# Cached keys turned in 32x32 blocks on VectorE and moved by transfers inside the chip, with a new order in the expert stream and in the sample softmax

## The chip, the cores and the metric

The kernel runs on one core of one Trainium2 chip, as one launch. The metric is the device time in microseconds (us) of that core. Three runs of the kernel before gave 1206.78, 1207.28 and 1207.90 us; their median is 1207.28.

## The reference, cut to what matters

One decoder layer for 256 prompt tokens and 8 sample tokens (one per sequence), width 1024, all in float32. Per layer: sparse attention beside a pooling mixer, cross-attention into 256 memory tokens, and a top-4-of-32 mixture of experts, each added to the residual.

```
# sample group, per sequence: 2048 cached keys in 16 pages, one new key
ki_past = cache_idx_k[page_table].reshape(DB, past, IDX_DIM)
s       = einsum('bqhd,bsd->bqhs', qi, ki) * IDX_DIM ** -0.5
score   = einsum('bqh,bqhs->bqs', w, relu(s))        # indexer score of each key
_, sel  = top_k(score, 256)                          # keys that may be attended
p       = softmax(where(valid, q . k[sel] * HEAD_DIM ** -0.5, NEG))
attn    = p @ v[sel]

# experts, for all 264 tokens
h    = tok @ w_up[e] + b_up[e]                       # 1024 x 2048 per expert
gate = minimum(h[:, :D], 7);  up = clip(h[:, D:], -7, 7)
out  = (gate * sigmoid(1.702 * gate) * (up + 1)) @ w_down[e] + b_down[e]
acc += combine[e][:, None] * out                     # combine is 0 where e is not in the top 4
```

The weights of an expert are 8 MiB (up) and 4 MiB (down); all 32 experts are computed.

## The kernel before, in words

Each engine has a program of its own, in an order written out by hand, and waits for the others on semaphores. Results of TensorE go to eight PSUM banks that are handed out in turn by the list `psum_jobs`: a job takes its bank (`take`) when the job eight places ahead of it has been copied out (`drained`), and announces its own end (`filled`). The order of that list is the order of TensorE's program.

**The front (0 to 280 us).** `w_in` is loaded in eight pieces, the seven projection tiles of `Z_FIRST` are computed, then the others (`z_tile`), each rotated by VectorE with the help of a swapped copy (`swap_halves` on TensorE, `rotate` on VectorE). Beside it the cached keys are made ready. A gather on GpSimd's queue (L623) brings a quarter `q` of the cached keys and indexer keys (two of 1 MiB) into `raw`; GpSimd copies the two side by side into `both` (L644, L646); TensorE turns `both` with 32 transposes of 128x128 per quarter (`turn_keys`, L782); ScalarE copies eight PSUM banks per quarter into `KT` (`keep_keys`). `sample_logits(c)` (L793) multiplies a quarter of the keys with the query heads, ScalarE takes the rectified values (`RL`) and the logits (`LG`), `sample_score(c)` (L801) sums the heads into scores, which ScalarE copies into `XS`. VectorE meanwhile finds the top 64 keys of each prompt token (accumulation at L1876 and L1878, then rounds of L1890 and L1892, first for token tile t = 0, then for t = 1, up to L1895), takes the prompt logits (L1919, L1928), and when all of `XS` is there, starts at L1964 a search for the 256th score in eight rounds (L1978), each with a small count on TensorE (L814). From its result `drop` a mask is spread over the heads by TensorE (`mb`, L966), added to the logits (L2010); one reduction over 2049 keys gives the maximum (L2019), one ScalarE instruction the exponentials with their sum (L1595), VectorE multiplies with the reciprocal (L2021, L2022), TensorE turns the probabilities (`spT`, L997) and multiplies them with the values (`spv`), and the output product `wo` (L1033), the memory attention and the router follow.

**The expert stream (from 280 us).** The weights of an expert come in six parts of 2 MiB (parts 0 to 3 up, 4 and 5 down). A ring of ten buffers (`RING`) holds them; the first ten parts are loaded during the front, wherever a buffer comes free. SyncE loads part `use + 10` when TensorE has read part `use` (`part_read`, `up_full`, `down_full`; L557 and L561 are the issues). TensorE's `expert` runs the up product (`up_rows`, L1258), gathers the next tokens (`gather_prompts`, L1201), turns the activations (L1236), adds the biases and sample tokens (L1209, L1215), runs the down product (`down_rows`, L1295) with the turned next tokens (L1223) inside it. Once per pair of experts, `spread_rows(0)` and `spread_rows(1)` (L1245) bring the finished rows of the pair before back to their tokens; they stand behind parts 0 and 1 of the even expert's up product, and VectorE adds them in `add_rows` (L2226), ahead of `activate`. `last_expert` turns the residual between its parts and spreads the rows of the expert before the last (`spread_before_last`, L1344), for tile r = 2 (8 rows) just ahead of the last down product. VectorE and ScalarE then norm and write the three tiles.

Of the kernel before, what the change touches and what calls it, by code (L numbers as in the profile page):

```python
# [25 lines left out]
P = 128  # L26
# [6 lines left out]
HD = 64  # L33
# [124 lines left out]
def psum_jobs():  # L158
    js = [("xT", k) for k in range(KD)]
    js += [("z", m) for m in Z_FIRST] + [("rs",)]  # L160
    js += [("z", 1), ("sw", 13), ("sw", 9), ("kin",), ("wr",)] + [("kt", i) for i in range(4)]
    js += [("z", 2), ("sw", 10), ("sw", 11)] + [("kt", i) for i in range(4, 8)]
    js += [("z", 3), ("sw", 12), ("sw", 4), ("sw", 0), ("kvn",), ("z", 5), ("sw", 1), ("sw", 2), ("sw", 3)]
    js += [("kt", i) for i in range(8, 12)] + [("is", 0, g, o) for g in range(2) for o in range(2)]
    js += [("z", 6)] + [("kt", i) for i in range(12, 16)] + [("is", 1, g, o) for g in range(2) for o in range(2)]
    js += [("z", 7), ("z", 8)]
    js += [("sl", 0)] + [("kt", i) for i in range(16, 24)]
    js += [("sl", 1), ("sc", 0)] + [("kt", i) for i in range(24, 32)]
    js += [("sl", 2)] + [("lg", 0, g, o) for g in range(2) for o in range(2)]
# [28 lines left out]
def build(nc, ins, outs, consts, ybuf):  # L198
# [6 lines left out]
    with ExitStack() as ctx:  # L205
# [119 lines left out]
        both = unit(14, 32, 2 * HD)  # L325
        KT = [unit(8, P, 32), unit(10, P, 32)]
# [174 lines left out]
        def _(sp):  # L501
# [26 lines left out]
            w_mk_rows = w_mk[0].rearrange("(k p) h e -> p k (h e)", p=P)  # L528
            wait_filled(sp, "sl", 3)
# [20 lines left out]
            load(vm, cache_mem_v[0].rearrange("b (t p) h e -> p b t (h e)", p=P), "vm_in")  # L550
            def load_part(use, e):
# [49 lines left out]
            for use in range(2):  # L601
                part_read(loops * BODY, use)
                load_part(use + RING, e)
# [12 lines left out]
        def _(pool):  # L616
# [12 lines left out]
            for q in range(4):  # L629
                gather(raw[:, 0].rearrange("p t d -> p (t d)"), cache_k, q, "raw_k")  # L630
                gather(raw[:, 1].rearrange("p t d -> p (t d)"), cache_idx_k, q, "raw_i")
                if q == 3:
                    wait_filled(pool, "z", 8)
                    for part in range(4):
                        gather(v_raw[:, 32 * part:32 * part + 32, :].rearrange("p t d -> p (t d)"), cache_v, part,
                               "raw_v")
                if q == 0:
                    for k in range(KD):
                        wait_filled(pool, "xT", k)
                else:  # L640
                    wait_filled(pool, "kt", 8 * q - 1)
# [5 lines left out]
                pool.wait_ge(S("side_by_side"), 2 * q + 2)  # L647
# [47 lines left out]
        def _(pe):  # L695
# [79 lines left out]
            def turn_keys(i):  # L775

                q = i // 8
                if i % 8 == 0:
                    pe.wait_ge(S("side_by_side"), 2 * q + 2)
                b = take(pe, "kt", i)  # L780
                for j in range(4):
                    ins = pe.transpose(b[:, j * P:(j + 1) * P], both[:, (4 * i + j) % 32, :], ident)  # L782
                done(ins, "kt", i)

            def sample_logits(c):
                for i in range(8 * c, 8 * c + 8):
                    wait_drained(pe, "kt", i)
                b = take(pe, "sl", c)
                for s in range(2):
                    for b4 in range(4):  # L790
                        n = 4 * s + b4
                        keys = KT[c % 2][:, n * NPG:(n + 1) * NPG, :].rearrange("p g t -> p (g t)")
# [25 lines left out]
            swap_halves(9)  # L818
            b = take(pe, "kin")
# [8 lines left out]
            for i in range(4):  # L828
                turn_keys(i)
            z_tile(2)  # L830
            swap_halves(10)
            swap_halves(11)
            for i in range(4, 8):
                turn_keys(i)
# [3 lines left out]
            swap_halves(0)  # L838
            b = take(pe, "kvn")
# [5 lines left out]
            z_tile(5)  # L845
            for m in (1, 2, 3):
                swap_halves(m)
            for i in range(8, 12):
                turn_keys(i)
# [5 lines left out]
            for i in range(12, 16):  # L855
                turn_keys(i)
            head_products("is", qiT, kiT, ki2, 1)
            z_tile(7)
            z_tile(8)
            pe.wait_ge(S("qb_ready"), 6)  # L860
            sample_logits(0)
            for i in range(16, 24):
                turn_keys(i)
            sample_logits(1)
            sample_score(0)
            for i in range(24, 32):
                turn_keys(i)
# [561 lines left out]
        def _(act):  # L1429
# [74 lines left out]
            for m in Z_FIRST + [1]:  # L1504
                keep_z(m)
# [818 lines left out]
```

## Time and profile before

| | us |
|---|---|
| median of three runs | 1207.28 |
| the profiled execution | 1206.73 |
| its span, first to last instruction | 1204.9 |
| PE busy | 1144.1 (95%) |
| DVE busy | 374.9 (31%) |
| ACT busy | 223.7 (19%) |
| POOL busy | 57.3 (5%) |
| mean granted TensorE clock | 0.995 |

PE is TensorE, PEld its weight loads, DVE VectorE, ACT ScalarE, POOL GpSimd, SP SyncE (SPq its DMA queue). A float32 matmul and a weight load count as two instructions each, a transpose as one. The device moved 451.92 MB, 374 GB/s over the span; in the slices from about 300 us to the end the page shows 426 to 430 GB/s, in those before 106 to 412 GB/s.

### The profile page before, as it was taken

How to read it: one execution, taken by the hardware profiler on the slowest of the kernel's cores; microseconds unless marked ns; L12 is line 12 of the kernel's file. 1: busy time of each engine (PE TensorE's matmuls, PEld its weight loads, DVE VectorE, ACT ScalarE, POOL GpSimd, SP SyncE). 2: the span in 40 equal slices, each digit the busy share in tenths (PEclk: the TensorE clock that was granted, in tenths of full speed). 3: DMA queues.
4: the chain of work that ended last, by engine and by line, in shares of the span. 5: the costliest groups of instructions: out<-in, count | busy, mean ns of one | idle time of the engine just before them, and what ended most of it. 6: DMA issues, size and time to landing. Idle time of an engine off the chain costs nothing.

```text
span 1204.9 us, 15008 instructions
## 1 busy us (share of the span) xinstructions
PE 1144.1 (95%) x5865; PEld 508.8 (42%) x5865; DVE 374.9 (31%) x888; ACT 223.7 (19%) x449; POOL 57.3 (5%) x71
## 2 busy tenths in 40 slices
PE   7998999999999999999999999999989898999997
PEld 6776568773333333333333333333323333333332
DVE  2279942534231322222222223122212222222222
ACT  2236641442111111111111111111111111111102
POOL 2138100000000000000000000000000000000000
PEclk9999999999999999999999999999999999999999
DMA  9345447797999999999999999999999999999994
GB/s 371 106 146 211 168 145 290 297 412 280 404 429 428 426 427 429 426 427 427 428 428 427 427 428 429 426 426 428 428 426 430 427 426 428 427 427 428 429 426 205
DMA packets 44245, 451.92 MB, mean 375 GB/s; under 512 B 5516, under 2 KB 6440, under 8 KB 18055
## 3 DMA queue, kind: packets, MB, share of 16 engines
q1 hardware_dynamic: 41695, 436.94, 86.7%
q0 software_dynamic: 2480, 14.02, 3.1%
q8 instruction: 47, 0.77, 0.3%
q14 instruction: 23, 0.19, 0.0%
HBM read 448.56 MB, written 2.61 MB: 374 GB/s over the span
## 4 chain that ended last, share of the span: by engine, by line
PE 59%; DMA 25%; DVE 12%; ACT 3%; issue 1%; SPq 0%; DVEq 0%; ACTq 0%
DMA mem<-in_w_up_dram 25%; PE psum L1258 20%; PE psum L1295 15%; PE psum L724 4%; PE psum L1245 3%; PE psum L1033 2%; DVE mem L2239 2%; PE psum L1209 2%; PE psum L931 1%; DVE mem L2231 1%; DVE mem L2234 1%; PE psum L1236 1%; ACT mem L1706 1%; DVE mem L2236 1%; PE psum L1223 1%
## 5 line engine op out<-in xcount | busy, mean ns | idle before, releaser
L1258 PE MATMUL psum<-mem 128*64 128x512 f32 x2048 | 457.4, 596 | 13.7 <-DMA mem<-in_w_up_dram 13.2
L1258 PEld LDWEIGHTS psum<-mem 128*64 128x64 f32 x2048 | 142.6, 137 | 303.8 <-issue 274.7
L1295 PE MATMUL psum<-mem 128*64 128x512 f32 x1024 | 236.9, 600 | 0.0
L1295 PEld LDWEIGHTS psum<-mem 128*64 128x64 f32 x1024 | 66.5, 136 | 133.2 <-issue 112.6
L2231 DVE TENSOR_SCALAR mem<-psum 128x512 f32<-128x512 f32 x32 | 22.2, 693 | 275.1 <-PE psum L1258 275.1
L1706 ACT ACTIVATE mem<-mem 128x512 f32<-128x512 f32 x32 | 20.2, 631 | 467.2 <-DVE mem L2231 467.2
L2226 DVE TENSOR_TENSOR mem<-mem,psum 128x528 f32<-128x528 f32 x64 | 45.2, 706 | 130.1 <-PE psum L1245 130.1
L1432 ACT ACTIVATE mem<-psum 128x512 f32<-128x512 f32 (+6 forms) x125 | 61.0, 550 | 97.6 <-PE psum L724 40.9
L1245 PE MATMUL psum<-mem 128*128 128x264 f32 x256 | 65.5, 398 | 0.0
L2216 DVE TENSOR_SCALAR mem<-mem 128x64 f32<-128x64 f32 x99 | 25.0, 312 | 126.9 <-PE psum L1230 99.4
L1201 PE MATMUL psum<-mem 128*64 128x512 f32 x256 | 60.4, 592 | 1.0 <-DVE mem L2147 1.0
L1245 PEld LDWEIGHTS psum<-mem 128*128 128x128 f32 x256 | 45.8, 188 | 32.5 <-issue 26.0
L724 PE MATMUL psum<-mem 128*128 128x264 f32 (+1 forms) x224 | 54.2, 403 | 0.7 <-DVE mem L1805 0.7
L2257 DVE COPY mem<-psum 64x512 f32<-64x512 f32 x30 | 20.5, 684 | 102.1 <-PE psum L1295 102.1
L724 PEld LDWEIGHTS psum<-mem 128*128 128x128 f32 (+1 forms) x224 | 43.2, 196 | 9.7 <-issue 1.1
L1716 ACT ACTIVATE mem<-psum 64x512 f32<-64x512 f32 x30 | 17.8, 595 | 118.7 <-PE psum L1295 118.7
L1708 ACT ACTIVATE mem<-psum 128x512 f32<-128x512 f32 x32 | 19.2, 599 | 104.3 <-PE psum L1236 104.3
L1236 PE MATMUL psum<-mem 128*128 128x128 f32 x128 | 21.0, 287 | 17.1 <-DVE mem L2239 17.1
L2239 DVE SCALAR_TENSOR_TENSOR mem<-mem 128x512 f32<-128x512 f32 x32 | 34.5, 1078 | 1.1
L1209 PE MATMUL psum<-mem 32*64 32x512 f32 x256 | 34.8, 613 | 0.0
L1215 PE MATMUL psum<-mem 8*64 8x512 f32 x128 | 34.4, 613 | 0.0
L1201 PEld LDWEIGHTS psum<-mem 128*64 128x64 f32 x256 | 18.3, 136 | 37.0 <-issue 37.0
(355 smaller groups left out, 859.8 us busy)
## 6 DMA issues: line engine op xcount, KB each, us to landing
mem<-in_w_up_dram SPq DMA_DIRECT2D x128, 2048.0 KB, 32.5
mem<-in_w_down_dram SPq DMA_DIRECT2D x64, 2048.0 KB, 33.8
mem<-in_w_in_dram SPq DMA_DIRECT2D x8, 868.0 KB, 15.5
mem<-in_cache_mem_k_dram SPq DMA_DIRECT2D x1, 4096.0 KB, 19.9
mem<-in_cache_mem_v_dram SPq DMA_DIRECT2D x1, 4096.0 KB, 15.0
mem<-in_w_o_dram SPq DMA_DIRECT2D x1, 3072.0 KB, 10.9
mem<-in_w_mk_dram SPq DMA_DIRECT2D x2, 1024.0 KB, 6.8
mem<-in_w_mv_dram SPq DMA_DIRECT2D x1, 2048.0 KB, 10.5
```

Source lines behind the costliest of these rows:

```text
L724: return pe.matmul(b[0:w, 0:NT], w_in_sb[k][:, m * P:m * P + w], xnT[:, k, :], start=(k == 0), stop=(k == KD - 1))
L1201: pe.matmul(psx[64 * o:64 * o + 64, :], slot_of[:, r, :], xn01[:, r, o * 512:(o + 1) * 512], start=(r == 0), stop=False, skip_group_check= ...
L1209: pe.matmul(ps[64 * o:64 * o + 64, :], esel[rows, :], ybias[rows, o * 512:(o + 1) * 512], start=True, stop=False, skip_group_check=True)
L1215: ins = pe.matmul(psx[64 * o:64 * o + 64, :], slot_of[0:TS, 2, :], etab[0:TS, o * 512:(o + 1) * 512], start=False, stop=True, skip_group_c ...
L1236: ins = pe.transpose(psa_t[:, c * P:(c + 1) * P], sig_b[:, c * P:(c + 1) * P], ident)
L1245: ins = pe.matmul(ps[:, 0:NT], outb[:, c * P:(c + 1) * P], ST[:, :], start=True, stop=True)
L1258: ins = pe.matmul(ps[64 * o:64 * o + 64, :], lhs, w[:, k % 2, g * 1024 + o * 512:g * 1024 + (o + 1) * 512], start=False, stop=(k == 7), sk ...
L1295: ins = pe.matmul(pso[64 * o:64 * o + 64, :], lhs, w[:, k % 4, o * 512:(o + 1) * 512], start=(k == 0), stop=(k == 7), skip_group_check=True)
L1432: ins = act.activation(out, in_, ACT.Copy)
L2226: dve.tensor_tensor(v, v, ps, ALU.add).then_inc(S("y_added"), 1)
L2231: dve.tensor_scalar(gate_b, banks[3], 7.0, None, ALU.min).then_inc(S("gate_ready"), 1)
L2239: dve.scalar_tensor_tensor(out=sig_b.rearrange("p (c q) -> p c q", c=4), in0=act_b.rearrange(turned, c=4), scalar=1.0, in1=gate_b.rearrang ...
```

## The change

1. **Keys.** `both`, GpSimd's eight copies, TensorE's 128 transposes and ScalarE's 32 copies go. `turn_blocks(q)` on VectorE turns each quarter of `raw` in 32x32 blocks into `blocks` (two instructions of 128x2048), and SyncE's queue moves it into `KT` with sixteen transfers per quarter, each of 32 partitions x 4 KiB, from partitions 32g to partitions 32b. `turn_blocks(0)` stands ahead of `rotate(13)`, (1) behind `rotate(9)`, (2) behind the copies into `QB`, (3) between the two prompt tiles of the top-64 search. The gather of quarter q waits for the blocks of q-1, the blocks of q wait for the transfers of q-1. TensorE's list is put in another order, with `sample_logits(0)` and `(1)` ahead of `z_tile(7)`.
2. **Sample softmax.** The maximum is taken in the four mask additions, the exponentials come in four pieces, TensorE turns each piece without waiting for the reciprocal, and ScalarE applies the reciprocal when it copies out the product with the values.
3. **Expert stream.** The spreads of finished rows go from parts 0 and 1 of the even expert's up product to behind the first and the second half of its down product (in the body; the last even expert keeps them: `early=True`). Biases and sample tokens are placed ahead of the turned activations, the turned next tokens ahead of the down product. The very first load of each pass of the body waits for half a part only (`row_read`) and comes in two halves; the last part comes in two halves with a semaphore of its own for the second. `spread_before_last(2)` goes behind the last down product.

```diff
+            for q in range(4):                                   # SyncE
+                sp.wait_ge(S("keys_turned"), 2 * q + 2)
+                if q >= 2:
+                    wait_filled(sp, "sl", q - 2)
+                for b4 in range(4):
+                    for g in range(4):
+                        sp.dma_start(KT[q % 2][32 * b4:32 * b4 + 32, g], blocks[32 * g:32 * g + 32, b4]
+                                     ).then_inc(S("keys_moved"), 16)
             wait_filled(sp, "sl", 3)
...
             for q in range(4):                                   # GpSimd
+                if q:
+                    pool.wait_ge(S("keys_turned"), 2 * q)
                 gather(raw[:, 0].rearrange("p t d -> p (t d)"), cache_k, q, "raw_k")
                 gather(raw[:, 1].rearrange("p t d -> p (t d)"), cache_idx_k, q, "raw_i")
-                pool.wait_ge(S("raw_k"), 16 * q + 16)
-                pool.tensor_copy(both[:, :, 0:HD], raw[:, 0]).then_inc(S("side_by_side"), 1)
-                pool.wait_ge(S("raw_i"), 16 * q + 16)
-                pool.tensor_copy(both[:, :, HD:2 * HD], raw[:, 1]).then_inc(S("side_by_side"), 1)
...
             def sample_logits(c):                                # TensorE
-                for i in range(8 * c, 8 * c + 8):
-                    wait_drained(pe, "kt", i)
+                pe.wait_ge(S("keys_moved"), 256 * (c + 1))
...
+            def turn_blocks(q):                                  # VectorE
+                for kind, name in enumerate(("raw_k", "raw_i")):
+                    dve.wait_ge(S(name), 16 * q + 16)
+                    if q:
+                        dve.wait_ge(S("keys_moved"), 256 * q)
+                    dve.transpose(blocks[:, 2 * kind:2 * kind + 2],
+                                  raw[:, kind].rearrange("p t (b d) -> p b t d", b=2)).then_inc(S("keys_turned"), 1)
...
-                dve.scalar_tensor_tensor(out=v, in0=v, scalar=HD ** -0.5, in1=b[:, :], op0=ALU.mult, op1=ALU.add
+                dve.tensor_tensor_reduce(v, v, b[:, :], HD ** -0.5, -FMAX, ALU.add, ALU.max, stat[:, 36 + c:37 + c]
...
-            act.activation(LG, LG, ACT.Exp, bias=stat[:, 0:1], accum_out=stat[:, 2:3]).then_inc(S("exp_s"), 1)
+            for c in range(4):
+                v = LG[:, c * 512:(c + 1) * 512 if c < 3 else NKEY]
+                act.activation(v, v, ACT.Exp, bias=stat[:, 0:1], accum_out=stat[:, 41 + c:42 + c]).then_inc(S("exp_s"), 1)
...
-            dve.tensor_scalar(LG, LG, stat[:, 2:3], None, ALU.mult).then_inc(S("prob_s_ready"), 1)
...
+                    if use == 0:                                 # SyncE, in the loop over the experts
+                        sp.wait_ge(S("row_read"), j + 1)
+                        load_half(later, e, 0, "slot0_in")
+                        part_read(j * BODY, 0)
+                        load_half(later, e, 1, "slot0_in")
+                        continue
...
             def expert(j, i, n, pair, early=False):              # TensorE
                 up_product(j, i, n, pair, early)
+                if i % 2 == 1 or early:
                     pe.wait_ge(S("y_added"), pair * 4 + 4)
                 gather_prompts(n + 2)
+                pe.wait_ge(S("gate_ready"), n + 1)
+                pe.wait_ge(S("up_clipped"), n + 1)
+                bias_rows()
+                gather_samples()
                 pe.wait_ge(S("act_ready"), n + 1)
                 turn_activations()
-                bias_rows()
-                gather_samples()
+                turn_tokens(n + 2)
                 pe.wait_ge(S("actt_copied"), n + 1)
-                down_part(j, i, 0, (0, 1))
-                turn_tokens(n + 2)
-                down_part(j, i, 0, (2, 3))
+                down_part(j, i, 0, (0, 1, 2, 3))
                 if i % 2 == 1:
                     turn_slots(gated)
+                elif not early:
+                    pe.wait_ge(S("xet_copied"), n + 2)
+                    finished_rows(n, pair, 0)
                 down_part(j, i, 1, (4, 5, 6, 7))
+                if i % 2 == 0 and not early:
+                    finished_rows(n, pair, 1)
...
-                down_part(j, 1, 1, (4, 5, 6, 7))                 # last expert
+                down_part(j, 1, 1, (4, 5))
+                pe.wait_ge(S("last_half_in"), 16)
+                down_part(j, 1, 1, (6, 7))
```

## Rows read from the trace of the kernel before

**Rows 1.** page part 4: shares of the span by line
```profile
DMA mem<-in_w_up_dram 25%; PE psum L1258 20%; PE psum L1295 15%; PE psum L724 4%; PE psum L1245 3%; PE psum L1033 2%; DVE mem L2239 2%; PE psum L1209 2%; PE psum L931 1%; DVE mem L2231 1%; DVE mem L2234 1%; PE psum L1236 1%; ACT mem L1706 1%; DVE mem L2236 1%; PE psum L1223 1%
```

**Rows 2.** chain of waits in order: start us, length us, what
```profile
338.45 3.43 PE psum L1258 x16
...
394.24 3.43 PE psum L1258 x16
...
1077.51 42.49 DMA mem<-in_w_up_dram
...
1136.25 43.09 DMA mem<-in_w_up_dram
```

**Rows 3.** DMA view: totals of 280:320, then of 320:360 us
```profile
DMA packets 851, 12.50 MB, mean 313 GB/s; under 512 B 87, under 2 KB 87, under 8 KB 87
...
DMA packets 1185, 17.11 MB, mean 428 GB/s; under 512 B 141, under 2 KB 141, under 8 KB 141
```

**Rows 4.** timeline of PE, first expert: start us, us, what, xcount
```profile
280.76 5.33 PE L1258 MATMUL psum<-mem 128*64 128x512 f32 x16
...
286.02 2.05 PE L1245 MATMUL psum<-mem 128*128 128x264 f32 x8
...
300.48 1.89 PE L1201 MATMUL psum<-mem 128*64 128x512 f32 x8
...
304.52 1.94 PE L1295 MATMUL psum<-mem 128*64 128x512 f32 x8
```

**Rows 5.** timeline of SP's DMA queue, 0 to 345 us
```profile
36.46 0.82 SPq L503 DMA_DIRECT2D out_dram<-in_state_pool_dram  x1
...
286.28 5.89 SPq L561 DMA_DIRECT2D mem<-in_w_down_dram  x2
```

**Rows 6.** timeline of PE, the last expert
```profile
1186.82 1.03 PE L1344 MATMUL psum<-mem 64*8 64x512 f32 x4
...
1187.77 7.09 PE L1295 MATMUL psum<-mem 128*64 128x512 f32 x32
```

**Rows 7.** DMA view, 1184:1194 us, GB/s in slices of 0.25 us
```profile
GB/s 377 213 131 459 131 328 197 328 279 98 410 229 279 279 66 197 246 246 213 279 49 49 66 16 33 16 33 0 0 0 0 0 0 0 0 0 0 0 0 0
```

**Rows 8.** timelines of PE and DVE in the sample softmax
```profile
162.83 5.42 PE L931 MATMUL psum<-mem 128*128 128x512 f32 x12
...
166.77 1.29 DVE L2022 TENSOR_SCALAR mem<-mem 128x2049 f32<-128x2049 f32 x1
```

**Rows 9.** timeline of DVE in the front
```profile
45.20 0.43 DVE L1823 TENSOR_TENSOR mem<-mem 8x264 f32<-8x264 f32 x1 [21.84 <-PE psum L741]
...
92.67 2.01 DVE L1895 SCALAR_TENSOR_TENSOR mem<-mem 128x128 f32<-128x128 f32 x1
...
110.00 2.34 DVE L1964 TENSOR_SCALAR_CACHE_REDUCE mem<-mem 128x2049 f32<-128x2049 f32 x1
```

**Rows 10.** waits of DVE, 45.2 to 110 us: us in total, times, longest
```profile
DVE mem L1825 <- PE psum L741: 10.9, 3, 4.3
...
DVE mem L1876 <- ACT mem L1501: 4.0, 1, 4.0
```

**Rows 11.** timeline of PE in the front
```profile
104.13 1.92 PE L793 MATMUL psum<-mem 128*32 128x512 f32 x16
```

**Rows 12.** page group of DVE over 2049 keys
```profile
L1978 DVE TENSOR_SCALAR_CACHE_REDUCE mem<-mem 128x2049 f32<-128x2049 f32 x7 | 16.4, 2349 | 0.3
```

**Rows 13.** b_up loads: GB/s in 65 ns slices from 148.4; landing
```profile
GB/s 441 441 315 315 504 378 189 0 0 0 252 63 189 504 315 63 315 441 126 252 189 252 63 315 189 189 189 252 0 0 0 0 0 0 0 0 0 0 0 0
...
DMA to landing us min/median/max: 2.4/2.4/2.5
```

**Rows 14.** PE by form, 14:16 and 30:38; clock ahead of DMA share, 282
```profile
L724 PE MATMUL psum<-mem 128*128 128x264 f32 x6 | 2.8, 647 | 0.0
...
L724 PE MATMUL psum<-mem 128*128 128x264 f32 x32 | 7.6, 386 | 0.0
...
282.00:283.00 1.00, 1.00 (x4) 0.24 (x2) 0.86 (x6) 0.93 (x1) 0.00 (x0) 0.50 0.09 25
```

More of the change, by code:

```diff
@@ L324, in build @@
         raw = unit(16, 2, 32, HD)
-        both = unit(14, 32, 2 * HD)
-        KT = [unit(8, P, 32), unit(10, P, 32)]
+        blocks = unit(14, 4, 32, 32)
+        KT = [unit(8, 4, 32, 32), unit(10, 4, 32, 32)]
         prob = [at(home(8), NH, P), at(home(8) + 1024, NH, TP)]
@@ L854, in _ @@
             z_tile(6)
-            for i in range(12, 16):
-                turn_keys(i)
             head_products("is", qiT, kiT, ki2, 1)
+            pe.wait_ge(S("qb_ready"), 6)
+            sample_logits(0)
+            sample_logits(1)
             z_tile(7)
             z_tile(8)
[L860 to L867, printed above, removed]
             sample_logits(2)
@@ L1261, in up_rows, with finished_rows, up_product @@
                 return ins
-            def up_product(j, i, n, pair):
+            def finished_rows(n, pair, half):
+                if half == 0:
+                    pe.wait_ge(S("rows_out"), n + 1)
+                    pe.wait_ge(S("rows_out2"), n + 1)
+                else:
+                    pe.wait_ge(S("y_added"), pair * 4 + 2)
+                spread_rows(half)
+            def up_product(j, i, n, pair, spreads):
                 pe.wait_ge(S("xet_copied"), n + 1)
@@ L1415, in _ @@
                     expert(j, i, j * BODY + i, j * (BODY // 2) + i // 2)
-            expert(loops, 0, loops * BODY, loops * (BODY // 2))
+            expert(loops, 0, loops * BODY, loops * (BODY // 2), early=True)
             last_expert(loops, loops * BODY + 1, loops * (BODY // 2))
@@ L1508, in _ @@
             copy(kin[0:TS, 2, :], b[0:TS, 144:216], "kin")
-            for i in range(4):
-                keep_keys(i)
-            keep_z(2)
-            for i in range(4, 8):
-                keep_keys(i)
             keep_z(3)
+            keep_z(5)
             b = result(act, "kvn")
@@ L1528, in _ @@
             keep_logits(0)
-            for i in range(16, 24):
-                keep_keys(i)
             keep_logits(1)
             keep_scores(0)
-            for i in range(24, 32):
-                keep_keys(i)
             keep_logits(2)
@@ L1706, in expert @@
                 act.activation(sig_b, gate_b, ACT.Sigmoid, scale=1.702).then_inc(S("sig_ready"), 1)
+                if not last:
+                    copy_tokens(n + 2)
                 act.wait_ge(S("actt_full"), n + 1)
@@ L1898, in _ @@
                     link(ins)
+                    turn_blocks(3)
                 else:
@@ L2245, in expert @@
                 e = dve.value_load(item_e[0:1, bass.ds(n + 2, 1)], min_val=0, max_val=NE - 1)
-                if b == 0:
-                    for m in range(4):
-                        add_rows(pair, m)
                 activate(n)
@@ L2255, in expert @@
                 assign_slots(n + 3, e)
+                if b == 0:
+                    add_rows(pair, 0)
+                    add_rows(pair, 1)
+                    dve.wait_ge(S("y_full"), pair * 4 + 4)
                 dve.wait_ge(S("down_full"), n + 1)
                 dve.tensor_copy(outb[64 * b:64 * b + 64, 0:512], banks[5][0:64, :]).then_inc(S("rows_out"), 1)
+                if b == 0:
+                    add_rows(pair, 2)
+                    add_rows(pair, 3)
             dve.wait_ge(S("list_ready"), 3)
```

136 lines of the change are left out of this document (59 added, 77 removed).

## The prediction

> **What bounds the kernel now.** I read the shares by line first: the largest step of the chain is the load of the up weights, and the products L1258 and L1295 come next, so the expert stream is the place [rows 1]. In the chain in order of time the reader is to see two regimes [rows 2]. From 338.45 to 394.24 us a pair of experts takes 55.8 us and every step is TensorE's. Late in the stream nearly a whole pair is one DMA step, and a pair takes 58.7 us (1077.51 to 1136.25): 12 parts of 2 MiB in 58.7 us are 428 GB/s. The DMA view shows that this rate is already there at 320 to 360 us [rows 3]. So the queue is full all the time; TensorE only lives on the ten parts loaded ahead until they are used up. What sets the end is (a) when the stream starts, (b) how long its queue runs empty in the first experts, (c) what follows the last up part, which lands at 1136.25 + 43.09 = 1179.3. A faster TensorE between 320 and 1130 us is worth nothing. From 280 to 320 us 12.50 MB moved, 29.2 us at 428 GB/s; so the queue ran as if it had started at 290.8 and never paused. Ahead of 280 us everything hangs on one serial chain; a shift s of it shifts all that comes later by s.
>
> **Expert stream.** The first part is read for 5.33 us and the first load goes out at 286.28 [rows 4, 5]. Now half a part is enough. These 16 instructions ran partly at the low clock (below), so I put their middle at 284.3, not at 283.4; the stream starts 1.9 us earlier. Then each spread of 2.0 us leaves parts 0 and 1, two in all [rows 4], so the parts 1, 2, 3 come free 2.0, 4.0, 4.0 us earlier, and the fourth the same. With 4.9 us of transfer per part (2.10 MB at 428) I ran through it: starts at 285.1, 290.6, 295.5, 300.4, 305.3, then 310.7 for the part that comes free at the end of the first down half (L1295 starts at 304.52 now, at 300.8 then) and the next; pauses 0.6 + 0.5 + 0.5 = 1.6 us. The stream is then as good as started at 285.1 + 1.6 = 286.7 instead of 290.8: **-4.1 us**. Bounds: 0 (the freed time is not used) and -5. The order inside `expert` (biases early, turned tokens ahead of the down product) is worth some 0.3 us of TensorE per expert, hidden behind the DMA queue: 0. The spreads in the down product and the later `add_rows` cost the same 4 us per pair as before; they sit behind `down_full` of the half that was read, so the queue is full when they come: 0. Only a pair of over 58.7 us would bring them into the sum, 3 us more than now.
>
> **Tail.** The last down product starts at 1187.77, behind a spread of 8 rows of 1.03 us [rows 6] that goes behind it: -0.95. It comes back in part, since tile 2 is then ready about when ScalarE wants it: +0.1. The last part lands before 1190.7, where the GB/s row falls to zero [rows 7]. Its first half would be wanted at 1190.4 and its second at 1192.1; with the two halves this fits. **-0.85**, bounds -1.0 and +0.5 (waits for the half).
>
> **Sample softmax.** Removed from VectorE: one pass for the maximum and one of 1.29 us for the scale. But behind the mask TensorE runs without a pause to 168.25 us on the memory values, then turns memory keys, and only then the probabilities, which were ready at 168.06 already [rows 8]. So the saving is off the path. VectorE now copies three of the four turned banks, ScalarE one: **-0.2**, bounds -0.6 and +0.5.
>
> **Keys.** This decides s. Before, VectorE reaches the search at 110.00 [rows 9], just when ScalarE copies the last score; both paths end together. Now they part.
>
> VectorE's path. From 45.20 to 110.00 it waited 14.9 us for TensorE's swapped tiles and for ScalarE [rows 10]; these go, as TensorE has 128 transposes less in that stretch, but 1.5 us of new waits for products I leave in. GpSimd's copies held VectorE three times: L1895 over 128 columns took 2.01 us instead of 0.35 [rows 9]; I count three such stalls (80.0, 92.7, 94.7), 4.9 us, gone. Added: three times two instructions over 2048 elements (the first quarter's two fit in the idle 21.84 us ahead of 45.20). No row shows a transpose; the nearest are 1.29 us (a multiply) and 2.35 us (a compare with a sum) per 2049 elements [rows 8, 12]. I take 2.2: 13.2 us; at 1.29 it would be 7.7. The Trainium skill says (Vector Engine (DVE) Microarchitecture Reference, on the reshape front end) that the 32x32 transpose sustains one element per cycle per lane; no run here shows it yet. The second quarter's blocks also wait for the first quarter's transfers: these go out at 37.3, when SP's queue is through [rows 5], and land at 49.4 (11.1 us as worked out below, and 1 us for the gather still under way) against 48.6, where `rotate(9)` ends: +0.8. Sum: 110.0 - 14.9 - 4.9 + 13.2 + 1.5 + 0.8 = 105.7. So VectorE alone would be 4.3 us earlier.
>
> The keys' path. Behind the fourth quarter's blocks VectorE has what it had from 94.7 to 110.0, less a stall: 13.8 us. So these blocks are done at 91.9. Then sixteen transfers of 128 KiB. No row has a transfer inside the chip of that size. The nearest are the two of `b_up`, also 32 partitions x 4 KiB: issued at 0.4 us each, 0.26 MB in 1.17 us (slices 11 to 28), so 224 GB/s, half the stream's 428; the first byte 1 us behind the issue, the landing 0.7 us behind the last [rows 13]. A quarter of 2.10 MB takes 9.4 + 1.7 = 11.1 us. At 428 GB/s it would be bound by the issues: 15 x 0.4 + 2.4 = 8.4 us. At half of `b_up`'s rate, if reading and writing the same SBUF count twice: 20.4 us. I take 11.1, and 1.5 us for the 4 MiB of values gathered at that time. A rule speaks against the change here: the Trainium skill (SBUF — State Buffer, Door 1: The DMA port swizzle) says that a run of 32 partitions reaches only half of the DMA ports, about 218 GB/s, and that transfers to the two halves in flight together hardly gain. The trace's 224 agrees; by the rule the quarter takes 11.3 us, by the full rate 8.4.
>
> So the keys are there at 91.9 + 11.1 + 1.5 = 104.5, hardly later than L793 starts now, 104.13 [rows 11], and from there 5.9 us to the search. But TensorE has been idle for over 10 us by then, and it wakes slowly: in 14 to 16 us, after the idle start, L724 took 647 ns, later 386; and at 282 us the granted clock was 0.50, that is 1.2 GHz, after the short waits for VectorE behind the router [rows 14]. The path holds 4.3 us of TensorE work, so between 0 and +4.3; I take +2.8, and 0.5 more for the values turned behind it. Search at 104.5 + 5.9 + 3.3 = 113.7: **s = +3.7**. From there on the chain is what it was. What goes on TensorE, ScalarE and GpSimd is not on this path.
>
> **Sum.** 3.7 - 4.1 - 0.85 - 0.2 = -1.45 us on the profiled execution of 1206.73: 1205.3. The median is 0.55 above that execution: **1205.8**.
>
> **Rivals.** Each is worked from the same sum.
> - Full rate: the transfers run at 8.4 us. Then no wait at 48.6 either, keys at 91.1 + 8.4 + 1.0 = 100.5, search at 109.7, s = -0.3: 1201.8. For it: sixteen transfers go to different partitions. Against: `b_up`. The same size of gain comes if the transpose costs 1.29 (s lower by 5.5: 1200.3); against it, that only plain one-input passes run that fast.
> - Slower than before: the transfers take more than 12.55 us per quarter, since s = T - 7.4 and 5.15 are to be paid back; more than 15 us is slower by over 2.4. Above 15 us VectorE itself starts to wait for the quarter before, three times over. At 20.4 us the four quarters run one behind the other: blocks 1 at 58.7, 2 at 83.5, 3 at 108.3, keys at 134.6, search at 143.8, s = +33.8: 1235.9. For it: source and target are the same memory, and gathers of 2 and 4 MiB share the queues. Against: nothing in the rows is under 200 GB/s at that shape.
> - The stream keeps its late start (the queue's pauses have another cause, or the half load saves nothing): -1.45 + 4.1: 1209.9. Against: the issue at 286.28 follows the end of part 0.
>
> **How the numbers follow.** My forecast has 0.50, with 1202.5 to 1209.5 as its own range (clock and shared queues, 3.5 us each way). Full rate or quick transpose 0.26, slow transfers 0.14, late stream 0.10. A measurement tells 0.2%, 2.4 us, from no change. Forecast: 0.13 faster, 0.30 same, 0.07 slower; full rate: 0.25 faster, 0.01 same; slow transfers: 0.14 slower; late stream: 0.02 faster, 0.04 same, 0.04 slower. Together 0.40, 0.35, 0.25. The range leaves out the slow end beyond 15 us and the best of the quick cases: 1199.5 to 1213.
>
> **What would show it.** In the trace after: the transpose's mean (2.2 us); the transfers' time from issue to landing and the GB/s of their stretch (some 220); the last `turn_blocks` ending near 92; L793's fourth run starting near 104.5 and taking more than 1.92 us at a low clock; the search starting near 113.7; the first load 2 us earlier behind the first product; 428 GB/s from then on; pairs of 58.7 us at the end; the last down product right behind the turned activations. I am wrong if the search starts ahead of 110, if the load stream is not at 428 GB/s, or if a pair takes over 59 us.

## The result and the profile after

Four runs of the changed kernel gave 1217.54, 1220.24, 1220.63 and 1220.68 us, median 1220.43, beside 1207.35 of the kernel before: a ratio of 1.0101, 95% interval 1.0086 to 1.0116. The change makes the kernel 12.2 us slower by this ratio (10.4 to 14.0), 13.1 by the medians. I had forecast 1205.8.

The profiled execution is the one of 1217.54 us, with a span of 1215.7 us, 10.8 more than before. Shares of the span by line; they answer to [rows 1] and look almost alike, which shows only that the stream still ends the kernel:

```profile
DMA mem<-in_w_up_dram 28%; PE psum L1249 21%; PE psum L1291 14%; PE psum L1233 4%; PE psum L1189 3%; SPq L532 3%; SPq L500 3%; PE psum L1021 2%; DMA mem<-mem 2%; PE psum L1197 2%; PE psum L919 1%; PE psum L1211 1%; PE psum L1135 1%; PE psum L1040 1%; ACT mem L1667 1%
```

New in it is SyncE's queue with L532, the sixteen transfers per quarter. VectorE's timeline in the front, kernel after (start us, length us, what, and in brackets the idle time before it with what ended it); it answers to [rows 9]:

```profile
51.34 4.50 DVE L1837 STREAM_TRANSPOSE mem<-mem 128x2048 f32<-128x2048 f32 x2 [4.64 <-DMA mem<-mem]
...
74.57 4.50 DVE L1837 STREAM_TRANSPOSE mem<-mem 128x2048 f32<-128x2048 f32 x2 [5.71 <-DMA mem<-mem]
...
100.58 4.50 DVE L1837 STREAM_TRANSPOSE mem<-mem 128x2048 f32<-128x2048 f32 x2 [6.56 <-DMA mem<-mem]
...
127.08 2.35 DVE L1971 TENSOR_SCALAR_CACHE_REDUCE mem<-mem 128x2049 f32<-128x2049 f32 x1 [8.33 <-ACT mem L1438]
```

Three times VectorE stands still, 16.9 us in all, until the transfers of the quarter before have landed. The fourth blocks are done at 105.1, and the search begins at 127.08: s = +17.1, where I had +3.7. TensorE's four runs of L793 and SyncE's queue in the same stretch; they answer to [rows 11] and [rows 5]:

```profile
72.49 1.93 PE L793 MATMUL psum<-mem 128*32 128x512 f32 x16
...
80.46 3.64 PE L793 MATMUL psum<-mem 128*32 128x512 f32 x16 [6.05 <-ACT mem L1502]
...
100.50 3.37 PE L793 MATMUL psum<-mem 128*32 128x512 f32 x16 [7.92 <-DMA mem<-mem]
...
120.05 3.64 PE L793 MATMUL psum<-mem 128*32 128x512 f32 x16 [13.17 <-DMA mem<-mem]
```

```profile
37.15 78.88 SPq L532 DMA_DIRECT2D mem<-mem  x64
...
299.77 1.89 SPq L560 DMA_DIRECT2D mem<-in_w_down_dram  x2
```

A quarter's transfers, from the turned blocks (for the first, from SyncE's first issue at 37.15) to their use, take 14.2, 18.8, 21.5 and 15.0 us. I had 11.1, and 12.6 for the fourth. The windows of 2 us in the first quarter (last three columns: granted clock, DMA share, GB/s) show the DMA engines full at half of the stream's rate:

```profile
40.00:42.00 2.00, 2.00 (x10) 1.71 (x10) 0.00 (x0) 0.00 (x0) 0.00 (x0) 1.00 0.92 210
42.00:44.00 2.00, 2.00 (x9) 1.13 (x9) 0.62 (x2) 0.39 (x1) 0.00 (x0) 1.00 1.02 213
44.00:46.00 2.00, 2.00 (x11) 1.71 (x10) 1.90 (x7) 0.00 (x0) 0.00 (x0) 1.00 0.99 213
```

The rest went as forecast or better. TensorE at the start of the stream and at its end, answering to [rows 4] and [rows 6]:

```profile
297.50 13.95 PE L1249 MATMUL psum<-mem 128*64 128x512 f32 x64
...
1197.62 1.04 PE L1338 MATMUL psum<-mem 128*8 128x128 f32 x8
1198.59 7.09 PE L1291 MATMUL psum<-mem 128*64 128x512 f32 x32
1206.47 1.99 PE L1429 MATMUL psum<-mem 64*128 64x512 f32 x8 [0.79 <-DVE mem L2295]
1208.39 1.03 PE L1346 MATMUL psum<-mem 64*8 64x512 f32 x4
```

The first product starts 16.7 us later than before and runs through without the spread that stood in it. The first load goes out 2.3 us behind its start, not 5.5. The last down product stands right behind the turned activations.

### The profile page after: what moved, and what is told of

The parts are those of the page before. It is cut to its first block, busy times and chain, and to the rows that moved or that the text cites. A ratio compares the mean times of both kernels' runs of the same rounds, so it can differ in the third digit from the quotient of the medians.

```text
span 1215.7 us, 14858 instructions
## 1 busy us (share of the span) xinstructions
PE 1133.2 (93%) x5736; PEld 499.1 (41%) x5737; DVE 381.9 (31%) x902; ACT 205.6 (17%) x422; POOL 40.7 (3%) x63
## 4 chain that ended last, share of the span: by engine, by line
PE 56%; DMA 30%; SPq 6%; DVE 4%; ACT 2%; issue 2%; DVEq 0%; ACTq 0%
DMA mem<-in_w_up_dram 28%; PE psum L1249 21%; PE psum L1291 14%; PE psum L1233 4%; PE psum L1189 3%; SPq L532 3%; SPq L500 3%; PE psum L1021 2%; DMA mem<-mem 2%; PE psum L1197 2%; PE psum L919 1%; PE psum L1211 1%; PE psum L1135 1%; PE psum L1040 1%; ACT mem L1667 1%
## 5 line engine op out<-in xcount | busy, mean ns | idle before, releaser
L1249 PEld LDWEIGHTS psum<-mem 128*64 128x64 f32 x2048 | 143.8, 137 | 318.8 <-issue 271.3
L1291 PEld LDWEIGHTS psum<-mem 128*64 128x64 f32 x1024 | 68.3, 137 | 121.6 <-issue 117.1
L1438 ACT ACTIVATE mem<-psum 128x512 f32<-128x512 f32 (+7 forms) x91 | 43.8, 529 | 103.2 <-PE psum L735 47.4
L1710 ACT ACTIVATE mem<-psum 64x512 f32<-64x512 f32 x30 | 17.8, 593 | 206.0 <-PE psum L1233 158.0
L735 PEld LDWEIGHTS psum<-mem 128*128 128x128 f32 (+1 forms) x224 | 43.4, 196 | 11.1 <-issue 2.4
L793 PE MATMUL psum<-mem 128*32 128x512 f32 x64 | 12.6, 929 | 27.1 <-DMA mem<-mem 21.1
L1189 PEld LDWEIGHTS psum<-mem 128*64 128x64 f32 x256 | 18.4, 137 | 37.0 <-issue 37.0
## 6 DMA issues: line engine op xcount, KB each, us to landing
mem<-in_w_o_dram SPq DMA_DIRECT2D x1, 3072.0 KB, 11.6
```

The costliest lines, as they stand in the source:

```text
L735: return pe.matmul(b[0:w, 0:NT], w_in_sb[k][:, m * P:m * P + w], xnT[:, k, :], start=(k == 0), stop=(k == KD - 1))
L1189: pe.matmul(psx[64 * o:64 * o + 64, :], slot_of[:, r, :], xn01[:, r, o * 512:(o + 1) * 512], start=(r == 0), stop=False, skip_group_check= ...
L1249: ins = pe.matmul(ps[64 * o:64 * o + 64, :], lhs, w[:, k % 2, g * 1024 + o * 512:g * 1024 + (o + 1) * 512], start=False, stop=(k == 7), sk ...
L1291: ins = pe.matmul(pso[64 * o:64 * o + 64, :], lhs, w[:, k % 4, o * 512:(o + 1) * 512], start=(k == 0), stop=(k == 7), skip_group_check=True)
L1438: ins = act.activation(out, in_, ACT.Copy)
```

## The experiments

Two theories on the transfers. **Path:** 32 partitions at either end can take or give only about half of the full rate, so the DMA engines are full at 205 to 220 GB/s. **Issue:** SyncE needs 0.635 us for each of the 64 issues, and 131 KB in 0.635 us are 206 GB/s. In the change the two numbers are the same, so its trace can't tell them apart. Each experiment is the changed kernel with the edit shown, unless it says otherwise. In the table, the first quarter's transfers run from the first issue to their use; where VectorE no longer waits for them, to their landing (e7) or to where the DMA share falls to zero (e10). The search started at 110.00 before. In e4, e7, e8, e9 and e10 the keys are not the reference's (parts are left out, or the blocks don't get to their places), so they are measurements of time and no kernels to use.

| run | median us | ratio to before, 95% interval | first quarter's transfers us | search start |
|---|---|---|---|---|
| the change | 1220.43 | 1.0101 (1.0086 to 1.0116) | 14.2 | 127.1 |
| e1_old_keys | 1205.73 | 0.9984 (0.9973 to 0.9995) | none | 112.5 |
| e2_keys_only | 1224.03 | 1.0134 (1.0116 to 1.0153) | as the change | 127.8 |
| e3_mixed_order | 1212.02 | 1.0042 (1.0031 to 1.0054) | 12.0 | 121.1 |
| e4_half_bytes | 1203.40 | 0.9963 (0.9951 to 0.9976) | 11.6 | 111.1 |
| e5_two_queues_mixed | 1217.35 | 1.0084 (1.0055 to 1.0113) | 12.3 | 125.2 |
| e6_two_queues_same_order | 1222.55 | 1.0124 (1.0106 to 1.0143) | 12.5 | 131.6 |
| e7_whole_transfer | 1199.90 | 0.9940 (0.9921 to 0.9958) | 8.8 | 109.2 |
| e8_one_gather | 1204.62 | one run | not read | 114.3 |
| e9_four_narrow | 1218.11 | one run | 13.5 | 127.3 |
| e10_four_wide | 1202.54 | one run | 8.1 | 108.6 |
| e11_act_copies_share | 1204.58 | 0.9977 (0.9967 to 0.9986) | off the path | 112.7 |
| e12_act_copies_half | 1201.18 | 0.9956 (0.9943 to 0.9970) | off the path | 108.3 |

**The parts alone.** e1 is the kernel before with the stream's, the tail's and the softmax's edits; e2 is the kernel before with the keys' edits.

> The kernel before with the stream's, the tail's and the sample softmax's edits, the keys turned on TensorE as before. The trace of the change has the stream 4.9 us shorter, the tail 1.0 us, the softmax 0.35 us, against 17.1 us that the search begins later. If these are separate terms: 1207.3 - 6.2 = 1201.1 us (1200 to 1202.5), search start 110.0. Rival: the stream is shorter only because it begins late (less beside it, a full ring): then 1205 to 1207.

> The kernel before with the new way of the keys alone; stream, tail and softmax as before. Separate terms: 1207.3 + 17.1 = 1224.4 us (1222 to 1227), search start 127.1. If the transfers cost less than that by themselves and the rest of the change is what is slow: under 1217.

e2 came as expected: +16.2 us (14.0 to 18.5) where the shift of the search is 17.8. So the loss is the keys' alone. e1 gained 1.9 us (0.6 to 3.3), where I had 6.2: a miss, and its time lies in the range of the rival that I wrote beside it, that the stream is shorter only because it begins late. e2's trace refutes that rival: its first product starts at 298.71, 18.0 us later than before, and from there to the end it takes 924.3 us with the old stream, 924.1 before. More on e1 is below. The two add up to +14.3, the change measured +12.2; the intervals meet.

**Order and bytes.**

```diff
-                for b4 in range(4):
-                    for g in range(4):
+                for i in range(4):                               # e3_mixed_order
+                    for b4, g in ((0, i), (2, (i + 2) % 4), (1, (i + 1) % 4), (3, (i + 3) % 4)):
...
-    sp.dma_start(KT[q % 2][32 * b4:32 * b4 + 32, g], blocks[32 * g:32 * g + 32, b4])
+    sp.dma_start(KT[q % 2][32 * b4:32 * b4 + 32, g, 0:16], blocks[32 * g:32 * g + 32, b4, 0:16])   # e4_half_bytes
```

> The changed kernel with the 16 transfers of a quarter in another order: four that follow each other read four different groups of 32 partitions and write four different ones (before: four in a row write the same 32 partitions). Theory path (the 32 partitions at either end can only take or give about half of the full rate, so 131 KB last 0.62 us and the queue backs up): an issue falls from 0.635 us to the 0.4 us of a load of the same kind, a quarter's transfers from 14.2 to about 10.5 us, search start 127 -> 113 to 118, time 1206 to 1212 us. Theory issue (SyncE needs 0.635 us for each, whatever it moves): nothing changes, 1217 to 1221 us.

> The changed kernel, each of the 64 transfers with half its bytes (65 KB in 32 rows of 2 KB); the other half of the keys is zeros written once at the start by GpSimd, so the keys are not the reference's. Theory path: an issue follows the bytes, 0.3 to 0.4 us, a quarter 14.2 -> 8.5 to 10 us, search start 107 to 115, time 1201 to 1209 us. Theory issue: 0.635 us each still, first quarter 13 to 14.2 us, the later ones a little shorter (less beside the gathers), 1214 to 1220 us.

The lines of the transfers in the first quarter (duration of the issue in ns, least, median and most; then first and last start) of the change, e3 and e4, with the time from issue to landing where the view gives it:

```profile
L532 SPq DMA_DIRECT2D mem<-mem x16: 584/592/885, 37.1 to 47.0; - x16
```

```profile
L532 SPq DMA_DIRECT2D mem<-mem x16: 590/595/622, 37.2 to 46.8; - x16
...
DMA to landing us min/median/max: 2.3/2.4/3.5
```

```profile
L533 SPq DMA_DIRECT2D mem<-mem x16: 585/591/622, 37.0 to 46.5; - x16
...
DMA to landing us min/median/max: 2.0/2.0/3.2
```

Neither theory passes whole. e4 came in at the time of the path theory (1203.4 us), but its first quarter took 11.6 us for 8.5 to 10; e3 came in at the edge of that theory's time (1212.0) with 12.0 us for 10.5. The issue takes 0.59 us with half the bytes and in any order, so 15 x 0.635 + 2 = 11.5 us is a floor for sixteen issues from one queue. But with half the bytes the engines are only half busy:

```profile
42.00:44.00 2.00, 2.00 (x9) 1.16 (x8) 0.27 (x1) 0.39 (x1) 0.00 (x0) 1.00 0.45 106
44.00:46.00 2.00, 2.00 (x11) 1.71 (x10) 1.87 (x7) 0.00 (x0) 0.00 (x0) 1.00 0.45 108
```

So 106 GB/s cost 0.45 of the engines here, and the full bytes all of them. Where the gathers run beside the transfers, that is what counts: the second and third quarter fell from 18.8 and 21.5 us to 14.1 and 15.6, and the time by 17 us, while the first quarter fell by only 2.6. The order is worth 2.2 us in the first quarter, 7 to 8 us of time in all.

**Two queues.** In e5 and e6 ScalarE issues every second transfer, in the mixed order and in the change's.

```diff
+        def move_keys(eng, q, moves):              # SyncE: MOVES[0::2], ScalarE: MOVES[1::2]
+            eng.wait_ge(S("keys_turned"), 2 * q + 2)
...
             for m in Z_FIRST:
                 keep_z(m)
+            move_keys(act, 0, MOVES[1::2])
```

> The changed kernel with the mixed order of e3_mixed_order and every second transfer issued by ScalarE. So far: an issue holds SyncE 0.635 us whatever it moves and in whatever order (0.59 with half the bytes too), and the last of 16 lands 4.6 us after its issue in the change's order, 2.4 in the mixed one. If both are terms: first quarter 12.0 -> 8 x 0.635 + 2.4 = 7.5 us (7 to 9), later quarters 18.3, 19.1, 12.9 -> 12 to 14, 13 to 15, 8.5, search start 121.1 -> 112 or less, time 1212.0 -> 1202 to 1205 us. If two queues share what one has (the DMA engines take 32-row transfers at this rate, whoever issues): first quarter 11 to 12, 1211 to 1213 us.

> As e5_two_queues_mixed, but in the change's order (four in a row write the same 32 partitions). Theory path and issue together: the issue is over after 5 us, but 2.1 MB go to 32 partitions at a time at 205 to 220 GB/s, so the first quarter is 9.5 to 10.5 us + 2 = 11 to 12.5 us (was 14.2), time 1210 to 1215 us. Theory issue alone: as the mixed order, 7.5 us and 1202 to 1205 us.

e5 refutes the first of its two forecasts (7.5 us): two queues share the full DMA engines. With the issues shared, the transfers still go at 217 to 250 GB/s, and the first quarter takes 12.3 us, about as the second forecast had it. Windows of e5, then of e6:

```profile
40.00:42.00 2.00, 2.00 (x11) 1.71 (x10) 0.00 (x0) 0.21 (x1) 0.00 (x0) 1.00 0.97 240
42.00:44.00 2.00, 2.00 (x10) 1.13 (x9) 0.00 (x0) 0.00 (x0) 0.00 (x0) 1.00 0.99 217
44.00:46.00 2.00, 2.00 (x10) 1.71 (x11) 1.87 (x6) 0.00 (x0) 0.00 (x0) 1.00 0.96 250
```

```profile
42.00:44.00 2.00, 2.00 (x10) 1.34 (x9) 0.00 (x0) 0.00 (x0) 0.00 (x0) 1.00 1.00 260
44.00:46.00 2.00, 2.00 (x10) 1.50 (x9) 1.48 (x4) 0.00 (x0) 0.00 (x0) 1.00 1.00 266
```

e6's first quarter took 12.5 us, at the end of its range of 11 to 12.5, but its time is 1222.6 us, over the forecast 1210 to 1215: its later quarters are again slower than e5's, the second 20.3 us for 17.4.

e5's time also lies over its forecast of 1211 to 1213. It costs 5.3 us against e3, since ScalarE now stands in its issues while others wait for its copies. Its timeline in e5 shows eight issues in 6.2 us ahead of the rectified products that VectorE works on:

```profile
76.02 6.17 ACTq L504 DMA_DIRECT2D mem<-mem  x8
82.58 0.66 ACT L1508 ACTIVATE mem<-psum 128x256 f32<-128x256 f32 x2 [18.84 <-issue]
```

The values' gather went out at 94.9, not at 89.2 as in e3, and met the fourth quarter's transfers, which took 17.3 us, not 12.9.

**Width.** The same bytes in one transfer (e7), in four of 32 rows x 16 KB (e9), in four of 128 rows x 4 KB (e10).

```diff
-                for b4 in range(4):
-                    for g in range(4):
-                        sp.dma_start(KT[q % 2][32 * b4:32 * b4 + 32, g], blocks[32 * g:32 * g + 32, b4])
+                sp.dma_start(KT[q % 2], blocks)                                                  # e7_whole_transfer
...
+                for g in range(4):                                                               # e9_four_narrow
+                    sp.dma_start(KT[q % 2][32 * (3 - g):32 * (3 - g) + 32], blocks[32 * g:32 * g + 32])
...
+                for g in range(4):                                                               # e10_four_wide
+                    sp.dma_start(KT[q % 2][:, g], blocks[:, g])
```

> The changed kernel with one transfer of 128 rows x 16 KB for each quarter in place of 16 of 32 rows; the blocks stay in their groups of partitions, so the keys are not the reference's. 2.1 MB at 420 GB/s are 5.0 us, + 2.4 of landing: first quarter 7.4 us (14.2), search start 111 to 114, time 1202 to 1206 us. If a transfer inside the chip goes at half the rate of a load however wide it is: 10 + 2.4 = 12.4 us, 1210 to 1214 us.

> The changed kernel with four transfers for each quarter, each of 32 rows x 16 KB from one group of 32 partitions to another (the blocks land in another place than they belong, so the keys are not the reference's). Against 16 of 32 x 4 KB it has a quarter of the issues and rows four times as long, and is as narrow. Seen so far: 32 rows x 4 KB go at 205 to 250 GB/s with the DMA engines busy, from one queue or two; 128 rows x 16 KB at 377 GB/s. Theory path (32 partitions at either end are too narrow): 205 to 250 GB/s, the first quarter's transfers 10 to 12 us. Theory row (a row of 4 KB costs an engine too much beside its bytes): over 350 GB/s, 8 to 9 us as in e7_whole_transfer.

> As e9_four_narrow, but each of the four transfers takes 4 KB of all 128 partitions (128 rows x 4 KB). Theory path: wide, so over 350 GB/s, the first quarter's 8 to 9 us, time 1200 to 1203 us. Theory row: the rows are as short as the change's, so 205 to 250 GB/s, 10 to 12 us.

Windows of the first quarter, first e9, then e10:

```profile
42.00:44.00 2.00, 2.00 (x9) 1.15 (x8) 0.25 (x1) 0.39 (x1) 0.00 (x0) 1.00 1.07 229
44.00:46.00 2.00, 2.00 (x11) 1.71 (x10) 1.87 (x7) 0.00 (x0) 0.00 (x0) 1.00 1.07 229
```

```profile
40.00:42.00 2.00, 2.00 (x11) 1.71 (x10) 0.00 (x0) 0.12 (x1) 0.00 (x0) 1.00 1.02 414
42.00:44.00 2.00, 2.00 (x9) 1.16 (x8) 0.05 (x1) 0.39 (x1) 0.00 (x0) 1.00 0.94 377
```

Four issues of 32 rows run at 229 GB/s and give 1218.1 us, about as slow as the change, without its issues; four issues of 128 rows run at 377 to 414 GB/s, with the same 4 KB rows as the change, and give 1202.5. The path is what counts, its width in partitions, and neither the row's length nor that source and target are the same memory. (e9's first quarter took 13.5 us, over the 10 to 12 that I had for it; its rate was in the range.)

One rival is left by the edits: e7 and e10 keep every row on its own partition, e9 does not. No run moves 128 rows between groups of partitions. Two rows speak against it: `b_up` comes from memory and goes to 32 partitions at 224 GB/s [rows 13], and in the change 4 of the 16 transfers of a quarter stay in their own group, while no slice of 0.18 us between 42 and 49 us is over 281 GB/s. Which of the two ends is the narrow one, source or target, these runs don't separate; `b_up` shows that a narrow target alone is enough.

The Trainium skill says (SBUF — State Buffer, Door 1: The DMA port swizzle) that a run of 32 partitions reaches half of the ports; 229 against 377 to 414 GB/s agree. It also says (same page, "Can I just issue two DMAs to hit both halves?") that two transfers to both halves in flight together hardly gain; e5, where SyncE's transfers go to the lower half of the partitions and ScalarE's to the upper, moves 233 GB/s from 40 to 48 us, and e6, where both write the same group of 32, moves 239: no gain, as the page says. Both are above the page's 218 GB/s for 32 partitions that the prediction went by; the change moved 210 in the same stretch.

**The gathers.**

```diff
             for q in range(4):                                   # e8_one_gather
                 if q:
-                    pool.wait_ge(S("keys_turned"), 2 * q)
+                    continue
```

> The changed kernel, where GpSimd gathers only the first quarter's keys and VectorE turns these four times; the keys of three quarters are left out. If the second and third quarters are slower than the first (18.8 and 21.5 us against 14.2) because the gathers run beside them: all four 14 to 15 us, search start 127 -> 115 to 118, time about 1207 to 1210 us. If it is the wait in the queue or a late start instead, they stay at 18 to 21.

VectorE waits nowhere for transfers, and the third quarter takes 13.5 us (69.8 to 83.33), not 21.5, with the change's own sixteen transfers. So 8 us of it were the gather beside it. The search starts at 114.3 (I had 115 to 118) and the time is 1204.6 us (1207 to 1210). The fourth takes 17.0 us, more than the change's 15.0: the gather of the values, left in, went out at 80.7 and ran in front of it.

**Fewer narrow bytes, the placement kept.** In the change ScalarE idled 23 us ahead of its first copy of a projection tile and for long stretches later, so it can move blocks itself.

```diff
+        ORDER = [(b4, g) for i in range(4) for b4, g in ((0, i), (2, (i + 2) % 4), (1, (i + 1) % 4), (3, (i + 3) % 4))]
+        BY_ACT = (8, 4, 4, 8)                    # e12_act_copies_half: (8, 8, 8, 8)
...
+            for b4, g in (ORDER[BY_ACT[q]:] if which == "sp" else ORDER[:BY_ACT[q]]):
+                if which == "sp":
+                    eng.dma_start(dst, src).then_inc(S("keys_moved"), 16)
+                else:
+                    eng.activation(dst, src, ACT.Copy).then_inc(S("keys_copied"), 1)
...
+            move_keys(act, "act", 0)             # and (1) behind keep_z(3), (2) behind keep_products(1), (3) behind keep_logits(1)
             for m in Z_FIRST + [1, 2]:
                 keep_z(m)
```

> The changed kernel with part of the blocks moved by ScalarE copies (8, 4, 4 and 8 of the 16 of the four quarters; ScalarE stood idle there), the rest by transfers in the mixed order. Issues of SyncE for a quarter: 8 x 0.635 = 5.1 us or 12 x 0.635 = 7.6, + 2.4 to land; 8 copies of 32x1024 at about 1.1 us, from the 128x512 copies of 0.6. Quarters: 17 (from 27, SyncE free at 37) , 11, 12 and 9 us (after: 14.2 behind SyncE, 18.8, 21.5, 15.0). Search start 109 to 112 (after 127.1, before 110.0), time 1200 to 1204 us. Rival: ScalarE's copies stand in the way of its other copies and VectorE waits (as with the second queue, e5_two_queues_mixed): 1207 or more.

> As e11_act_copies_share, with 8 of the 16 blocks of every quarter copied by ScalarE. In e11 the DMA engines were full from 56 to 66 us (the third quarter's gathers beside 12 narrow transfers) and again from 76 to 88, and VectorE idled 3.8 and 1.6 us before it turned the third and fourth quarter. Four transfers less in each: 4 x 0.6 = 2.4 us of full DMA engines less, twice. If DMA time is what these quarters wait for: search start 112.7 -> 109 to 111, time 1204.6 -> 1201.5 to 1203.5 us. If ScalarE's 4.3 us more in the queue ahead of its other copies is worth as much: 1204 to 1207 us.

ScalarE's copies in e12, then VectorE's turns:

```profile
27.03 8.60 ACT L511 ACTIVATE mem<-mem 32x1024 f32<-32x1024 f32 x8 [13.69 <-DVE mem L1853]
...
53.83 8.59 ACT L511 ACTIVATE mem<-mem 32x1024 f32<-32x1024 f32 x8
...
75.57 8.58 ACT L511 ACTIVATE mem<-mem 32x1024 f32<-32x1024 f32 x8
...
89.61 8.60 ACT L511 ACTIVATE mem<-mem 32x1024 f32<-32x1024 f32 x8 [2.80 <-DVE mem L1853]
```

```profile
65.44 4.50 DVE L1853 STREAM_TRANSPOSE mem<-mem 128x2048 f32<-128x2048 f32 x2 [0.36 <-issue]
...
85.07 4.50 DVE L1853 STREAM_TRANSPOSE mem<-mem 128x2048 f32<-128x2048 f32 x2
...
108.31 2.35 DVE L1987 TENSOR_SCALAR_CACHE_REDUCE mem<-mem 128x2049 f32<-128x2049 f32 x1 [5.43 <-ACT mem L1449]
```

VectorE's waits for transfers are gone, the search begins 1.7 us earlier than in the kernel before, and e12 is 5.3 us faster (0.9956, 0.9943 to 0.9970). It beats both kernels. Against e11 it gains 3.4 us by the medians and 2.5 us by the two ratios, whose intervals just touch. e11 ended a little over its forecast (search 112.7 for 109 to 112, 1204.6 us for 1200 to 1204), e12 a little under (108.3 for 109 to 111, 1201.2 for 1201.5 to 1203.5).

## Why the prediction was wrong, point by point

**The step that failed: "A quarter of 2.10 MB takes 9.4 + 1.7 = 11.1 us", and "1.5 us for the 4 MiB of values".** It is a mis-sized term of a mechanism that was named. The rate was right (224 forecast, 205 to 215 measured). Three things were missing:
- `b_up` is two transfers. Its issue of 0.4 us is 0.635 here, and its landing 2.4 us behind the last issue is 4.6 here in the change's order, where narrow transfers to one group queue up, and 2.4 in the mixed one (e3). 15 x 0.635 + 4.6 = 14.1, and 14.2 is measured.
- Narrow bytes fill the DMA engines like nearly twice as many wide ones (0.99 to 1.02 of them at 213 GB/s in the change, 0.94 at 377 in e10). I counted the values' gather beside the fourth quarter with 1.5 us and forgot the gathers of the next quarter's keys beside the second and third: 18.8 and 21.5 us. e8 takes 8 us of it away.
- VectorE waits for the transfers of the quarter before. I had said so in the rival, for quarters above 15 us, and given the rival 0.14; of 16.9 us of such waits I had 0.8 in the sum. The limit was too high as well: the first quarter's 14.2 us cost 4.6, since `rotate(9)` was through at 46.7 and not at 48.6.

In the sum: the fourth blocks at 105.1 for 91.9 (+13.2: +16.1 of waits, and -2.9 since the rest of VectorE's path was faster than I had it), the last transfers 15.0 for 12.6 (+2.4), from there to the search 7.0 for 9.2 (-2.2). That is the 13.4 us between +3.7 and +17.1. The rival's formula s = T - 7.4 would have given 7.6 for the fourth quarter's T = 15; it held only while one quarter's transfers decide, and here all four did.

**The turn itself** was right: 2.2 us forecast; 2.29 measured, kernel after, all of the front behind 30 us:

```profile
L1837 DVE STREAM_TRANSPOSE mem<-mem 128x2048 f32<-128x2048 f32 x6 | 13.5, 2290 | 16.9 <-DMA mem<-mem 16.9
```

**TensorE's slow wake** was right in kind: the fourth run of L793 took 3.64 us for 1.92 behind 13.2 us of idling, and the granted clock was 0.50, that is 1.2 GHz, from 120 to 122 us. The path from there took 7.03 us for 5.9, +1.1, where I had +2.8 and 0.5.

**GpSimd's stalls** went as forecast. L1895 had taken 2.01 us [rows 9]; it is L1901 now (0.29 us over 128 columns, the other form has 256):

```profile
L1901 DVE SCALAR_TENSOR_TENSOR mem<-mem 128x128 f32<-128x128 f32 (+1 forms) x2 | 0.7, 360 | 0.1
```

In e1, where GpSimd still copies, the same instruction takes 2.00 us.

**Softmax:** from the search to the stream 170.42 us for 170.76, -0.34; forecast -0.2.

**Stream and tail.** From the first product to the end of the span, worked out from the rows of each profile:

| | before | after | e1 | e3 | e7 | e12 |
|---|---|---|---|---|---|---|
| first product to first load | 5.52 | 2.27 | 3.82 | 3.81 | 3.08 | 2.25 |
| to the last down product | 901.5 | 898.8 | 900.1 | 899.3 | 899.1 | 900.4 |
| to the end | 17.1 | 17.1 | 17.1 | 17.2 | 17.1 | 17.1 |
| sum against before | | -5.9 | -3.1 | -3.9 | -4.8 | -4.4 |

I had -4.95 (4.1 + 0.85). These five are not all: worked out the same way, e4 gives -2.1, e5 -5.6, e6 -2.2, e8 -4.4, e9 -4.4, e10 -2.5 and e11 -3.7. The mean of the twelve profiles with the new stream is -3.9, so the change's own -5.9 is the best of them and the forecast was 1 us too high. The tail is in the second row: the last up part lands 24.57 us ahead of the end for 25.56, -1.0 for -0.85. Half the part does free the first load early. By how much hangs on the granted clock as the first product starts: the 64 instructions of the up product took 13.95 us in the change and in e12, 15.64 in e1, 15.65 in e3. The second row spreads by 2.4 us, 898.8 to 901.2, over the twelve, and no run shows why.

**e1's miss** has two known parts. Its stream gained 3.1 us, not 5.9. And its search began at 112.46 though its program up to there is the kernel before's: its granted clock was 0.69 to 0.89 at 44 to 52 us and 0.57 at 64 to 68, where before had 1.00. How much of the 2.5 us these dips made was not tested. Its ten runs lie between 1202.8 and 1206.8. Whether the unprofiled ones had such dips, no record shows; nor does one show why three of the change's four runs were 3 us above the profiled one. That stays open.

## What to carry to other kernels

Count a transfer by how many partitions it spans: 32 rows went at 229 GB/s and kept all DMA engines full, 128 rows at 377 to 414, so a block move between groups of 32 partitions takes nearly double its bytes from every transfer beside it. When transfers replace work of an idle engine, write down for each what else is in the DMA queues at that moment, and check the case in which each waits for the one before, with all of them in the sum. If an engine stands idle there, let it copy part of the blocks: with half of them on ScalarE the kernel went from 12 us slower to 5 us faster than before, the stream's gain of some 4 us included.

## What the runs showed of the hardware

- The issue of a transfer inside the chip held SyncE for 0.59 us with 131 KB and with 65 KB, and ScalarE, beside SyncE's issues, for 0.67 us (median of the 32 in e5; 0.89 in the first quarter), where a load of `b_up` took 0.4.
- Transfers inside the chip from 32 partitions to 32 moved 210 GB/s from 40 to 48 us in the change, 221 in e9, 233 in e5 and 239 in e6, with the DMA engines 95% busy or more; with half the bytes (e4) it was 106 to 111 GB/s at 0.45 to 0.47.
- A transfer inside the chip over 128 partitions ran at up to 414 GB/s, near the 428 of the loads from memory.
- ScalarE copied 32 partitions x 1024 float32 from one group of partitions to another in 1.07 us (8.60 for 8), and VectorE's turns beside it stayed at 2.25 us each.
- The granted clock fell towards 0.50, the lower level of 1.2 GHz, in stretches in one profile and not in another with the same instructions there; eight products of `gather_prompts` ahead of the stream took 3.55 us in e1 and 1.94 in the change.
